# Probabilities times values in plain float32: one matmul per key tile in place of three rounded ones

## The reference

```python
# nsa_mixer: two softmax attentions over the same queries, one on the "selected" keys, one on the "window" keys
s = jnp.einsum('bqghd,bgqnld->bghqnl', qc, kg) * scale
p = masked_softmax(s, mask)
o_slc = jnp.einsum('bghqnl,bgqnld->bqghd', p, vg)
...
o = g[:, :, 0] * o_cmp + g[:, :, 1] * o_slc + g[:, :, 2] * o_win
# fox_mixer: causal attention with a decay term added to the scores
s = jnp.einsum('bqhd,bkhd->bhqk', qc, k) * scale
s = s + Fq[..., None] - F[:, :, None, :]
p = masked_softmax(s, mask)
return jnp.einsum('bhqk,bkhd->bqhd', p, v)
```

## Time and profile before

| | |
|---|---|
| median of three runs | 1847.43 us |
| span of the profiled execution | 1849.7 us |
| TensorE matmul records, busy | 1781.5 us (96%), 8160 |
| TensorE weight loads, busy | 1344.1 us (73%), 8160 |
| DVE busy | 1059.8 us (57%) |
| ACT busy | 867.4 us (47%) |
| POOL busy | 144.1 us (8%) |
| DMA | mean 64 GB/s |
| TensorE clock granted, mean | 0.979 of full speed |

### The profile page before, as it was taken

The page is one execution under the profiler, slowest core; times in us unless marked ns, Lnnn a source line. Parts: engine busy times, 40 slices in busy tenths (PEclk is TensorE's granted clock), DMA queues, the critical chain, the costliest instruction groups (busy, mean ns, idle before and its releaser), DMA issues.

```text
span 1849.7 us, 26742 instructions
## 1 busy us (share of the span) xinstructions
PE 1781.5 (96%) x8160; PEld 1344.1 (73%) x8160; DVE 1059.8 (57%) x2636; ACT 867.4 (47%) x1841; POOL 144.1 (8%) x170
## 2 busy tenths in 40 slices
PE   5999999999999999999969999999999999999997
PEld 3767777777777777888847777777777777688885
DVE  6467777765545555333465777777555554543344
ACT  3566666654444444222236666665444444432222
POOL 3121111100000000000023111111000000000000
PEclk8989999999999999999979999999999999999998
DMA  7220101012212123333432101011112221233331
GB/s 187 61 58 24 35 24 35 24 44 56 63 46 65 49 57 103 92 101 95 121 102 68 35 24 35 24 35 35 47 46 69 51 63 46 57 122 94 99 94 68
DMA packets 223875, 118.05 MB, mean 64 GB/s; under 512 B 20128, under 2 KB 220832, under 8 KB 223264
## 3 DMA queue, kind: packets, MB, share of 16 engines
q1 hardware_dynamic: 219104, 107.66, 21.8%
q0 software_dynamic: 1216, 8.65, 1.2%
q10 hardware_dynamic: 3456, 0.54, 0.2%
HBM read 110.41 MB, written 6.42 MB: 63 GB/s over the span
## 4 chain that ended last, share of the span: by engine, by line
PE 80%; ACT 7%; DVE 7%; issue 4%; POOL 1%; ACTq 1%; DVEq 0%; POOLq 0%
PE acc L1295 51%; PE o_pair L1381 9%; PE scores L1345 6%; PE turned L1358 5%; PE scores L1344 3%; ACT kk_hi L701 2%; PE scores L1349 2%; ACT w_hi L646 2%; ACT q_swap L682 1%; ACT prob L763 1%; DVE w_lo L929 1%; PE o_pair L1411 1%; PE misc L1396 1%; PE turned L1467 1%; DVE prob L1046 1%
## 5 line engine op out<-in xcount | busy, mean ns | idle before, releaser
L1295 PE MATMUL acc<-h_hi,w_hi 128*128 128x512 f32 (+1 forms) x1152 | 473.4, 411 | 30.0 <-DVE h_lo L431 24.1
L1295 PE MATMUL acc<-h_hi,w_lo 128*128 128x512 f32 (+1 forms) x1152 | 465.3, 404 | 0.0
L1295 PE MATMUL acc<-h_lo,w_hi 128*128 128x512 f32 (+1 forms) x1152 | 463.5, 402 | 0.0
L763 ACT ACTIVATE prob<-prob,row_max 128x128 f32<-128x128 f32 (+3 forms) x384 | 214.8, 559 | 270.1 <-DVE row_max L1027 268.1
L929 DVE TENSOR_TENSOR w_lo<-w_raw,w_hi 128x1024 fp32r<-128x1024 f32 x192 | 233.5, 1216 | 147.0 <-ACT w_hi L646 144.4
L1295 PEld LDWEIGHTS acc<-h_hi,w_hi 128*128 128x128 f32 (+1 forms) x1152 | 215.8, 187 | 101.8 <-DVE h_lo L431 29.4
L646 ACT ACTIVATE w_hi<-w_raw 128x1024 fp32r<-128x1024 f32 x192 | 199.7, 1040 | 180.2 <-PE acc L1295 176.1
L1295 PEld LDWEIGHTS acc<-h_hi,w_lo 128*128 128x128 f32 (+1 forms) x1152 | 216.1, 188 | 65.4 <-issue 21.4
L1295 PEld LDWEIGHTS acc<-h_lo,w_hi 128*128 128x128 f32 (+1 forms) x1152 | 216.3, 188 | 56.5 <-issue 16.1
L1027 DVE CUSTOM_DVE_ANT_0 prob<-scores,causal 128x128 f32<-128x128 f32 (+3 forms) x384 | 186.3, 485 | 118.3 <-PE scores L1349 55.0
L772 ACT ACTIVATE pt_hi<-turned 128x128 fp32r<-128x128 f32 (+3 forms) x384 | 165.1, 430 | 174.2 <-PE turned L1358 169.9
(11 more groups left out here) (156 smaller groups left out, 2066.4 us busy)
## 6 DMA issues: line engine op xcount, KB each, us to landing
w_raw<-in_w_in_dram SPq DMA_DIRECT2D x140, 512.0 KB, 3.8
w_raw<-in_w_proj_nsa_dram SPq DMA_DIRECT2D x16, 512.0 KB, 3.6
w_raw<-in_w_proj_fox_dram SPq DMA_DIRECT2D x16, 512.0 KB, 3.6
w_raw<-in_w_out_dram SPq DMA_DIRECT2D x16, 512.0 KB, 3.5
x_scratch<-xT POOLq DMA_DIRECT2D x2, 2048.0 KB, 9.2
xT<-x_scratch POOLq DMA_DIRECT2D x2, 2048.0 KB, 8.2
x_nat<-in_x_dram SPq DMA_DIRECT2D x2, 1024.0 KB, 6.7
c_w<-in_cmp_w_k_dram SPq DMA_DIRECT2D x4, 512.0 KB, 7.6
```

The lines of the kernel that those rows point to most:

```text
L763: act.activation(prob[:, ring, 0:width], prob[:, ring, 0:width], ACT.Exp, bias=row_max[:, ring:ring + 1], scale=-1.0, accum_out=row_sum[:, ...
L1295: ins = pe.matmul(acc[par][0:width, :], w[:, par, k, 0:width], rhs, start=(n == 0), stop=(n == 23))
```

## The change

`v_hi` and `v_lo` become one float32 tile `v_all` with 192 columns per tile (64 zeros, 64 values, 64 zeros), and `pt_hi` and `pt_lo` one float32 tile `pt`; unnamed tiles keep the places of the others. ACT's two copies stay and write float32, DVE's two subtractions go. One wait on `pt_done` or `v_done`, signalled by ACT, stands where one on DVE's `pt_lo_done` or `v_lo_done` stood. `value_step` issues one float32 matmul per key tile, 512, 384, 256 and 128 queries wide, with a stationary operand of 128 columns for both heads. The closing matmul of a fox pair is in float32 too. GpSimd clears two strips of `v_all` as before, and one strip of `pt` where it cleared two.

```diff
-            v_hi = sb("v_hi", [P, 2, 2, QT, 2 * HD], F32R)
-            v_lo = sb("v_lo", [P, 2, 2, QT, 2 * HD], F32R)
-            pt_hi = sb("pt_hi", [P, 2, PT_COLS], F32R)
-            pt_lo = sb("pt_lo", [P, 2, PT_COLS], F32R)
+            v_all = sb("v_all", [P, 2, 2, QT, 3 * HD])
+            sb("place_of_xT_rest", [P, 2, T])
+            pt = sb("pt", [P, 2, PT_COLS])
+            sb("place_of_norm_rest", [P, 2, PT_COLS])
...
-                for pt in (pt_hi, pt_lo):
-                    pool.memset(pt[:, :, 3 * 384 + 2 * P:3 * 384 + 3 * P].bitcast(F32), 0.0).then_inc(pads, 1)
+                pool.memset(pt[:, :, 3 * 384 + 2 * P:3 * 384 + 3 * P], 0.0).then_inc(pads, 1)
...
-                    act.activation(pt_tiles(pt_hi, a, qt), turned_tiles(s, qt), ACT.Copy)\
-                        .then_inc(pt_hi_done, 1)
+                    act.activation(pt_tiles(pt, a, qt), turned_tiles(s, qt), ACT.Copy)\
+                        .then_inc(pt_done, 1)
...
-            def v_rest(n, to, hi):
-                dve.wait_ge(v_hi_done, n + 1)
-                dve.tensor_tensor(to, misc[:, :].rearrange("p (k s d) -> p s k d", k=QT, s=2), hi,
-                                  ALU.subtract).then_inc(v_lo_done, 1)
...
-                def lo_step(pair, s):
-                    a, qt = divmod(s, QT)
-                    dve.wait_ge(pt_hi_done, pair.s0 + s + 1)
-                    dve.tensor_tensor(pt_tiles(pt_lo, a, qt), turned_tiles(s, qt), pt_tiles(pt_hi, a, qt),
-                                      ALU.subtract).then_inc(pt_lo_done, 1)
...
-                    if step(LAG_PT):
-                        lo_step(*step(LAG_PT))
...
                     if s >= 2 or prev is not None:
-                        pe.wait_ge(pt_lo_done, pair.s0 + s - 1)
+                        pe.wait_ge(pt_done, pair.s0 + s - 1)
...
-                    pe.wait_ge(pt_lo_done, pair.s0 + QT * (a + 1))
+                    pe.wait_ge(pt_done, pair.s0 + QT * (a + 1))
...
-                    width = (HD, P)[h]
                     last = a == pair.steps // QT - 1
                     for kt in range(QT):
-                        q0 = min(P * kt, T - 2 * P)
-                        for m, (v, pt) in enumerate(((v_hi, pt_hi), (v_hi, pt_lo), (v_lo, pt_hi))):
-                            ins = pe.matmul(o_pair[0:width, q0:T], v[:, b, stream, kt, 2 * HD - width:2 * HD],
-                                            pt[:, a % 2, 384 * kt + q0:384 * kt + T],
-                                            start=not pair.nsa and (a, kt, m) == (0, 0, 0),
-                                            stop=pair.nsa and last and (kt, m) == (QT - 1, 2))
+                        q0 = P * kt
+                        ins = pe.matmul(o_pair[:, q0:T], v_all[:, b, stream, kt, HD * (1 - h):HD * (3 - h)],
+                                        pt[:, a % 2, 384 * kt + q0:384 * kt + T],
+                                        start=not pair.nsa and (a, kt) == (0, 0),
+                                        stop=pair.nsa and last and kt == QT - 1)
                     if last and not pair.nsa:
-                        zeros = pt_hi[:, a % 2, 3 * 384 + 2 * P:3 * 384 + 3 * P]
-                        ins = pe.matmul(o_pair[:, 0:P], v_hi[:, b, stream, 0, :], zeros, start=False, stop=True)
+                        zeros = pt[:, a % 2, 3 * 384 + 2 * P:3 * 384 + 3 * P]
+                        ins = pe.matmul(o_pair[:, 0:P], v_all[:, b, stream, 0, 0:P], zeros, start=False, stop=True)
```

More of the change, by code:

```diff
@@ L336, in bass_trunk @@
         v_turned = sem("v_turned")
-        v_hi_done = sem("v_hi_done")
-        v_lo_done = sem("v_lo_done")
+        v_done = sem("v_done")
         c_landed = sem("c_landed")
@@ L359, in bass_trunk @@
         s_turned = sem("s_turned")
-        pt_hi_done = sem("pt_hi_done")
-        pt_lo_done = sem("pt_lo_done")
+        pt_done = sem("pt_done")
         pv_mm = sem("pv_mm")
@@ L611, in _ @@
                 apart(pool)
-                for v in (v_hi, v_lo):
-                    flat = v[:, :, :, :, :].rearrange("p b s k c -> p (b s k) c")
-                    pool.memset(flat[:, :, 0:HD].bitcast(F32), 0.0).then_inc(pads, 1)
+                flat = v_all[:, :, :, :, :].rearrange("p b s k c -> p (b s k) c")
+                for edge in (0, 2 * HD):
+                    pool.memset(flat[:, :, edge:edge + HD], 0.0).then_inc(pads, 1)
                 pool.memset(c_blk[:, :, :, :, N_CMP:N_PAD].rearrange("p a j g n -> p (a j g) n"),
@@ L714, in v_round @@
                 act.activation(to, misc[:, :].rearrange("p (k s d) -> p s k d", k=QT, s=2),
-                               ACT.Copy).then_inc(v_hi_done, 1)
+                               ACT.Copy).then_inc(v_done, 1)
             def z_tanh_of(half, par, r, b):
@@ L865, in _ @@
                 act.wait_ge(x_saved, 16 * (l + 1))
-                v_round(l * 10, v_hi[:, :, 0, :, HD:2 * HD])
+                v_round(l * 10, v_all[:, :, 0, :, HD:2 * HD])
                 split_hi(*kv(10))
@@ L870, in _ @@
                 z_tanh_of(*kv(9), 2 * PAIRS * l, 0)
[L871 removed]
+                v_round(l * 10 + 1, v_all[:, :, 1, :, HD:2 * HD])
                 bodies(act, l, body)
@@ L1014, in body @@
                         at(plan.at_end(1, 1), lambda: k_rest(acc[1], places, n + 1, False))
-                        at(plan.at_end(2, 2), lambda: v_rest(v, v_lo[:, proj.b, :, :, HD:2 * HD],
-                                                             v_hi[:, proj.b, :, :, HD:2 * HD]))
                         at(plan.at_end(3, 1), lambda: z_silu_of(*proj.unit(3), proj.r, proj.b))
@@ L1194, in _ @@
                 dve.tensor_tensor(f_lo[:, :], f_b[:, :], f_hi[:, :], ALU.subtract).then_inc(f_step, 1)
-                v_rest(l * 10, v_lo[:, :, 0, :, HD:2 * HD], v_hi[:, :, 0, :, HD:2 * HD])
                 split_lo(*kv(10))
@@ L1198, in _ @@
                 z_silu_of(*kv(9), 2 * PAIRS * l, 0)
-                v_rest(l * 10 + 1, v_lo[:, :, 1, :, HD:2 * HD], v_hi[:, :, 1, :, HD:2 * HD])
                 dve.wait_ge(gates_done, 2 * l + 2)
@@ L1326, in turn @@
                         if not att.nsa:
-                            pe.wait_ge(v_lo_done, v)
+                            pe.wait_ge(v_done, v)
                         turn_v(v, q_raw)
@@ L1373, in value_step @@
                             pe.wait_ge(y_mul, pair.r + 2)
-                        pe.wait_ge(v_lo_done, l * 10 + 2 + (0 if pair.nsa else pair.i + 1))
+                        pe.wait_ge(v_done, l * 10 + 2 + (0 if pair.nsa else pair.i + 1))
                     h, b, stream, _ = pair.atts()[a]
-                    width = (HD, P)[h]
                     last = a == pair.steps // QT - 1
                     for kt in range(QT):
-                        q0 = min(P * kt, T - 2 * P)
-                        for m, (v, pt) in enumerate(((v_hi, pt_hi), (v_hi, pt_lo), (v_lo, pt_hi))):
-                            ins = pe.matmul(o_pair[0:width, q0:T], v[:, b, stream, kt, 2 * HD - width:2 * HD],
-                                            pt[:, a % 2, 384 * kt + q0:384 * kt + T],
-                                            start=not pair.nsa and (a, kt, m) == (0, 0, 0),
-                                            stop=pair.nsa and last and (kt, m) == (QT - 1, 2))
+                        q0 = P * kt
[3 more added lines that the diff above has]
+                                        stop=pair.nsa and last and kt == QT - 1)
                     if last and not pair.nsa:
-                        zeros = pt_hi[:, a % 2, 3 * 384 + 2 * P:3 * 384 + 3 * P]
-                        ins = pe.matmul(o_pair[:, 0:P], v_hi[:, b, stream, 0, :], zeros, start=False, stop=True)
+                        zeros = pt[:, a % 2, 3 * 384 + 2 * P:3 * 384 + 3 * P]
+                        ins = pe.matmul(o_pair[:, 0:P], v_all[:, b, stream, 0, 0:P], zeros, start=False, stop=True)
                     ins.then_inc(pv_mm, 1)
@@ L1392, in cmp_scores @@
                     pe.wait_ge(cb_ready, 4 * (l + 1))
-                    pe.wait_ge(v_lo_done, l * 10 + 2)
+                    pe.wait_ge(v_done, l * 10 + 2)
                     apart(pe)
@@ L1474, in _ @@
                     kv(n)
-                pe.wait_ge(pads, 2 + 5 * l + 3)
+                pe.wait_ge(pads, 2 + 4 * l + 3)
                 pe.wait_ge(c_landed, 160 * (l + 1))
@@ L1500, in _ @@
                 kv(9)
-                pe.wait_ge(v_lo_done, l * 10 + 1)
+                pe.wait_ge(v_done, l * 10 + 1)
                 turn_v(l * 10 + 1, z_silu[:, 1, :])
-                pe.wait_ge(pads, 2 + 5 * l + 5)
+                pe.wait_ge(pads, 2 + 4 * l + 4)
                 apart(pe)
```

2 lines of the change are left out of this document (1 added, 1 removed).

## The result

The changed kernel takes 1855.08 us (median of 5 runs, 1854.35 to 1859.17) against 1847.43 us (5 runs): ratio 1.0051, 95% interval 1.0035 to 1.0066, so 6.5 to 12.2 us slower.

The account below looks back on a forecast made before the run. TensorE, its instructions issued back to back, was taken to bound the attention. 27.3 for matmuls + 3 for seams - 7.6 for pauses, less 1.5 for small waits, came to +21 us: 1868.5 us, range 1860 to 1877.

Parts of the forecast that it names:

- The step of 2.15 us: TensorE's value step in float32: eight records, 2.15 us, or 2.26 with the 0.11 us open weight load after scores.
- the 27.3 of the sum: TensorE's added time over 96 longer value steps and 16 closing matmuls of fox pairs: +27.3 us.
- rival (b): Granted clock falls to 1.2 GHz behind the float32 value steps: about 2060 us; chance 0.02.
- (c): Not slower: float32 passes overlap or stream at one clock per column, 67 us gained, 1780 us; chance 0.03 together with (e).
- (e): The float32 matmul is made in one rounded pass, with the outcome of (c); chance 0.03 together with (c).
- the seams: Between a value step's float32 matmuls: 0.01 us on three seams of each of 96 steps, +3 us.
- the small waits: TensorE's many small waits on DVE, under the rows' resolution: 1.5 us taken off, bounds 0 and 3.
- the two pauses: TensorE's nsa pauses, after the second head 0 step (0.33) and before the next pair's scores (0.21), both go: -7.6 us.
- Rival (a): The pauses stay, because ACT takes DVE's place as the late engine: +30, 1877 us; chance 0.08.
- The bottom of the sum: Low end of the forecast of +13 to +29: 27.3 - 2 - 7.6 - 3 - 1.4.
- The -5 at the top of the sum: Last term of the forecast's high end, 27.3 + 7 - 5, for +29.
- Rival (d): No difference: DVE's relief is worth more than the two pauses, needing 15 us more, 0.16 per value step; chance 0.03.

Follow-up runs that it names:

- Experiments 1 and 2: First: changed kernel with DVE's subtractions put back, results unread, 1869.8 us. Second: kernel before without DVE's 384 subtractions for the probabilities, 1829.4 us.
- experiment 7: Kernel before with last key tile in float32 (128 stationary columns), and DVE's weight remainder ahead of the probabilities' in each fox body's sixth slot: 1832.0 us, ratio 0.9918.
- experiment 1: Changed kernel with DVE's removed subtractions computed again into tiles nobody reads, TensorE waiting for them: 1869.8 us, ratio 1.0122 to the kernel before.
- experiment 3: Changed kernel with head 0's stationary operand back at 64 columns: 1865.9 us, ratio 1.0099 to the kernel before.
- experiment 5: Kernel before with plain float32 for the last key tile alone, 64 stationary columns for head 0: 1841.7 us, ratio 0.9970.
- experiment 4: Kernel before with DVE making the remainder of the probabilities after each slot's other work, not ahead of it: 1919.0 us, ratio 1.0402.
- The run with both edits: Kernel before with the last key tile in float32 and DVE's remainder of the probabilities after each slot's other work: 1922.5 us, ratio 1.0409.

## Why the prediction was wrong, point by point

**Right: what bounds the kernel, and the price of the steps.** TensorE from start to start is the time of the attention, before and after. The step of 2.15 us, and 2.26 behind scores, came out as 2.15 and 2.26; the closing matmul at +0.16 for +0.17. Per pair that is 1.06 and 0.64 us, 27.2 over 32 pairs, for the 27.3 of the sum. ACT's copies, costed at nothing, kept their length with a float32 output (430 and 431 ns in the mean). The clock did not fall in the value steps, so rival (b) is out, and so are (c) and (e), as the records are two per matmul at two clocks per column.

**The step that failed, 5.6 us: a third recurring pause, put at nothing.** The part on DVE's relief named two pauses and called the rest small. The fox pause of 0.40 us on `w_lo` was in the same wait view of the kernel before, right above the one that was quoted from it as the one of note:

```profile
PE acc L1295 <- DVE w_lo L929: 5.0, 16, 0.8
```

The prediction took up one wait on a tile that the change doesn't touch, `q_st`, and left this one out without a reason. A relieved engine also brings its other work earlier. Experiments 1 and 2 bring the 14 pauses back and take them away with the subtractions, and experiment 7 takes them away by order alone.

**Wrong, 3 us: the seams.** The sum put 0.01 us on three seams of each step, between a lower bound of 0 and 0.02. They cost nothing: 2.26 us is the sum of the records and the one open load.

**Too small, 1 us: the small waits.** The sum took off 1.5 us for them. Of the 15.7 us between TensorE's +27.3 and the attention's +11.6 the three pauses are 13.2, which leaves 2.5. This is by difference; no row itemises it.

**Right in size, half right in cause: the two pauses.** 7.6 us came back. But one of the two was covered by the longer step and not removed by relief, as experiment 1 shows. The prediction had both reasons side by side and did not tell them apart. Rival (a), that the pauses stay, did not happen.

**The rest.** 27.3 + 3 - 7.6 - 1.5 was +21. Without the seams (3), with 5.6 less for the third pause and 1.0 less for the small waits it is +11.6, what the attention shows at full clock, and the measured 6.5 to 12.2 contains it. The bottom of the sum, +13.3, had the seams at 0 already; it allowed 3 us for all waits that were not itemised, and 5.6 lay in one. The -5 at the top of the sum is not worked out from a row. Rival (d) had the direction of the error, DVE's relief worth more than the two pauses, and was given 0.03; its price was taken as all or nothing, where half of it happened.

## What to carry to other kernels

Where one engine sets the time, price its instructions from start to start, and then list every wait of that engine that the change can move, those on untouched work of the relieved engine too: a removed instruction brings forward all that stands behind it in its queue. A pause can vanish because its cause is gone or because the waiting engine is now late itself; only the first is a gain that a faster step would keep. A reordering helps in the slot where the waiting engine stands and can cost far more elsewhere (5 us gained against 4% lost here). Use full float32 by tile: on the widest tiles three rounded passes are cheaper (0.69 against 0.86 us at 512 columns), on the tile of 128 that had to be widened to 256 the one float32 matmul is (0.22 against 0.35).

## What the runs showed of the hardware

A plain float32 matmul with 64 stationary columns leaves weight loads open: 0.09 us behind its last record (experiment 3), and 0.09 to 0.10 ahead of its first one behind rounded records of 64 columns (experiment 5) or of 128 (the fox pairs of experiment 3). With 128 columns neither gap is there, though the one open load behind half-height scores is 0.05 longer. Rounded matmuls of 64 columns have no such gap. No run shows why.

The granted clock fell to half at the start of the attention in one profiled execution of the kernel before, for 10.2 us, and not in another. A difference of 5 us between two single profiles of this kernel can be this alone. When the order of DVE's queue made TensorE wait 62 times (experiment 4), the clock also fell to half within the attention, for 51 us in all, which added about half as much again to what the waits cost. The run with both edits, with 62 such waits too, had 61 us of it there.
